# Last pair of heads of a mixed convolution/attention layer: projection units cut in halves earlier and spread over more steps

## What is computed

```
z = u_lat @ w_in                              # B, C, X, G (1024 columns each), Q, K, V, BG
y_a = z[B] * dwconv(z[C] * z[X], w_conv, 1)   # short convolution over tokens
y_a = y_a * silu(z[G])
y_b = neighbourhood_attention(q, k, v, k_ctx, v_ctx, rpb) * silu(z[BG])
y_lat = concatenate([y_a, y_b]) @ w_out
```

## Time and profile before

| | |
|---|---|
| median of 3 runs | 2403.7 us (2403.24 to 2404.94) |
| the profiled execution's own time | 2403.63 us |
| its span in the trace | 2401.8 us |
| PE busy | 2261.0 us, 94% |
| DVE, ACT, POOL busy | 63%, 49%, 22% |
| step 5 of the last pair to the end of its block | 1222 to 1291.5 us |

### The profile page before, as it was taken

One profiled execution on the slowest core, in us unless ns is written; L12 is line 12 of the kernel. 1 busy time (PEld: TensorE's weight loads), 2 busy tenths in 40 slices (PEclk: granted clock), 3 DMA queues, 4 the chain that ended last, 5 costly groups with the idle time before them and its releaser, 6 DMA issues. The chain is left out here.

```text
span 2401.8 us, 33875 instructions
## 1 busy us (share of the span) xinstructions
PE 2261.0 (94%) x12000; PEld 1966.3 (82%) x12000; DVE 1501.9 (63%) x2368; ACT 1188.4 (49%) x1714; POOL 528.3 (22%) x303
## 2 busy tenths in 40 slices
PE   4799999999999999999997999799999999995998
PEld 3688888888888888888885888688998999894887
DVE  5167575774757757576576436557766776667444
ACT  4244434444344443444444334366777678767322
POOL 1333132331322313223230300022212221220300
PEclk8899999999999999999998999899999999997999
DMA  6212211221112211122116555111111111114654
GB/s 247 62 35 68 63 57 33 68 72 59 57 33 73 71 55 57 33 81 63 55 27 226 163 167 175 55 40 53 53 52 54 53 53 58 48 53 140 218 154 144
DMA packets 165352, 199.79 MB, mean 83 GB/s; under 512 B 51064, under 2 KB 125944, under 8 KB 162168
## 3 DMA queue, kind: packets, MB, share of 16 engines
q1 hardware_dynamic: 155304, 174.53, 23.2%
q10 hardware_dynamic: 9792, 23.07, 2.7%
q0 software_dynamic: 144, 0.52, 0.1%
HBM read 166.11 MB, written 31.98 MB: 82 GB/s over the span
## 5 line engine op out<-in xcount | busy, mean ns | idle before, releaser
L950 PE MATMUL ps<-u_hi,w_hi 128*128 128x512 f32 (+1 forms) x1536 | 559.5, 364 | 16.6 <-POOL w_lo L637 16.6
L950 PE MATMUL ps<-u_hi,w_lo 128*128 128x512 f32 (+1 forms) x1536 | 545.2, 355 | 0.0
L950 PE MATMUL ps<-u_lo,w_hi 128*128 128x512 f32 (+1 forms) x1536 | 544.1, 354 | 0.0
L950 PEld LDWEIGHTS ps<-u_hi,w_hi 128*128 128x128 f32 x1536 | 290.6, 189 | 54.1 <-POOL w_lo L637 16.7
L950 PEld LDWEIGHTS ps<-u_hi,w_lo 128*128 128x128 f32 x1536 | 290.3, 189 | 41.9
L950 PEld LDWEIGHTS ps<-u_lo,w_hi 128*128 128x128 f32 x1536 | 291.2, 190 | 37.3
L1525 POOL TENSOR_TENSOR o_w_lo<-o_w_raw,o_w_hi 128x1024 fp32r<-128x1024 f32 x48 | 138.8, 2891 | 669.5 <-ACT o_w_hi L1540 669.5
L1795 PE MATMUL ps<-u_hi,o_w_hi 128*128 128x426 f32 (+2 forms) x640 | 238.0, 372 | 13.9 <-POOL o_w_lo L1525 9.3
L742 ACT ACTIVATE probs<-probs,neg_max 128x640 f32<-128x640 f32 (+1 forms) x160 | 122.8, 768 | 251.5 <-DVE neg_max L858 250.4
L637 POOL TENSOR_TENSOR w_lo<-w_stage,w_hi 128x1024 fp32r<-128x1024 f32 x64 | 153.4, 2397 | 418.6 <-ACT w_hi L695 418.6
L656 POOL TENSOR_TENSOR bias_tile<-bias_piece,col_mask 128x384 f32<-128x384 f32 x128 | 142.7, 1118 | 440.0 <-DVE neg_max L858 439.9
(11 more groups left out here) (176 smaller groups left out, 4274.6 us busy)
## 6 DMA issues: line engine op xcount, KB each, us to landing
y_tile<-y_scratch SPq DMA_DIRECT2D x72, 512.0 KB, 5.1
w_stage<-in_w_even SPq DMA_DIRECT2D x64, 512.0 KB, 3.7
o_w_raw<-in_w_odd SPq DMA_DIRECT2D x48, 512.0 KB, 3.6
ada_piece<-in_w_ada SPq DMA_DIRECT2D x16, 1024.0 KB, 5.7
wout_raw<-in_w_out SPq DMA_DIRECT2D x16, 1024.0 KB, 10.1
ada_pieces<-in_w_ada SPq DMA_DIRECT2D x4, 2048.0 KB, 18.3
y_scratch<-h_backward SPq DMA_DIRECT2D x16, 512.0 KB, 2.7
h_scratch<-h_tile ACTq DMA_DIRECT2D x18, 256.0 KB, 2.3
```

The lines of the kernel that those rows point to most:

```text
L950: last = nc.tensor.matmul(ps[:, bank(j, g), 0:t - f], w[:, slot, c * P:(c + 1) * P], x[:, c, f:t], start=(c == 0 and n == 0), stop=(c == K ...
```

## The change

For the last pair alone: whole units in steps 0 to 4 instead of 0 to 7, half units (4 of the 8 chunks) in steps 5 to 18 instead of 8 to 15. Step 19 has none. The convolution store moves from step 16 to step 19.

```diff
+LAST_WHOLE = 5
...
-        if s < 8:
+        if s < LAST_WHOLE:
             return [(*ORDER[s], 0, KC)]
-        if s < LAT_STEPS:
-            return [(*ORDER[8 + (s - 8) // 2], s % 2 * (KC // 2), (s % 2 + 1) * (KC // 2))]
+        if s < STEPS - 1:
+            n, part = divmod(s - LAST_WHOLE, 2)
+            return [(*ORDER[LAST_WHOLE + n], part * (KC // 2), (part + 1) * (KC // 2))]
         return []
...
-                    if s == (LAT_STEPS if last else 13):
+                    if s == (STEPS - 1 if last else 13):
                         act.wait_ge(ya_done, i + 1)
                         store_conv(act, i)
```

## The result

| | before | changed |
|---|---|---|
| median | 2403.47 us (2402.37 to 2404.94, 6 runs) | 2412.51 us (2410.36 to 2413.4, 6 runs) |
| the profiled execution's own time | 2403.63 | 2412.11 |
| mean granted clock of PE | 0.977 | 0.974 |

The ratio is 1.0033 with a 95% interval of 1.0023 to 1.0042: the change costs 9.0 us. The forecast was 6.3 us more, 2409.9. The direction and the place were right; the time is 2.6 us above the forecast and 0.7 us above the upper end of the range that the prediction gave.

A forecast was written before the change was run, and what follows sets the result against it. PE, busy for 94% of the span, bounds the kernel; DVE's last output and its store set the block's end. Exposed loads delay the border 6.3 us: 2403.63 + 6.3 = 2409.9 us, range 2406.3 to 2411.8.

The forecast's parts named there:

- main term: Block's border: CG2 done 7.0 us later, the weight loads' transfer exposed, and the block left 6.3 us later.
- 15.45 to 16.8: Block's border: us from CG2's end, when the loads are issued, until all stores have landed.
- The step keeps its 7.66: Step 7: DVE's L841 meets POOL's split of G's weights again, so the step takes 7.66 us, as step 6 did before.
- rival 3: Step 7: POOL's next bias tile runs first after the split, DVE waits 1.1 us more; 2411.0 us, chance 0.10.
- Steps 8, 9 and 10: 3 x 4.58: Steps with halves of CB0 and CB1 take 4.58 us each, 13.74 in all.
- the steps' gain: Last pair: weigh(19) comes at 1284.55 instead of 1286.30, 1.75 us earlier.
- On SP's queue behind them: Block's border: the attention store, issued at about 1287 behind the four loads on SP's queue, waits for them.
- From the same state ... at half its clock: Behind the border: work starts in the same order and state, PE at half clock, so 6.3 us carry to the end.
- Rival 1: Block's border: the store of y does not wait for the loads, the kernel is 1.75 us faster; 2401.9 us, chance 0.07.
- rival 2: Step 7: L841 begins before POOL's split, so the step takes 5.9 us instead of 7.66; 2408.1 us, chance 0.12.
- Rival 4: Last pair: steps come out 1.5 to 3 us shorter in all than forecast; 2407 to 2408.4 us, chance 0.11.
- steps 12, 16 and 17: Last pair's steps without a profile row of their own, taken as 4.1, 3.9 and 4.05 us.

The follow-up runs named there:

- before_late_loads: The kernel before, steps untouched, with SP issuing the four output weight loads only after output(17): 2411.11 us, ratio 1.0027.
- lw7: The changed kernel with whole units in steps 0 to 6, halves in steps 7 to 16, convolution store in step 17: 2404.27 us, ratio 0.9999 to the kernel before.
- split_late: The changed kernel with POOL's split of G's weights behind bias tile 10 instead of 8 in the last pair: 2410.86 us, ratio 1.0028.
- act_store: The changed kernel with the last pair's attention store issued on ACT's queue instead of SP's: 2411.7 us, ratio 1.0035.
- lw7_two_p1late: lw7 with two of four loads behind the next block's first y load, the next four behind y of tiles 2 and 3: 2401.3 us, ratio 0.9989.

## Why the prediction was right, and where it was off

- **The main term held.** CG2 done later, the loads later, their transfer exposed, the block left later. before_late_loads brings 7.4 of the 9.0 us with this alone by the medians, 5.9 of 9.3 by its trace; lw7, whose loads come 52.33 us behind weigh(5) where before it was 51.85, loses nothing. "15.45 to 16.8" for the time to the last landing was 15.83.
- **"The step keeps its 7.66" was mis-sized.** It was 8.27, as rival 3 had said: the bias tile was ready when the split ended and met the two L845. They took 1.73 us instead of the 1.01 that split_late shows without POOL beside them. The Trainium skill, "SBUF — State Buffer", section "SBUF: two separate sides", gives operations of DVE with two SBUF inputs as ones that can be kept waiting by GpSimd; the 1.73 agrees, and this is the case of three in a row that the trace of before did not have. The price was 0.6 to 0.7, not the 1.1 of the rival.
- **"Steps 8, 9 and 10: 3 x 4.58" failed for step 8,** 6.20. I had seen that the smaller filling becomes idle time in step 7, and had costed that idle time at nothing. It was 3.52 us, and the clock fell behind it. Steps 9 and 10 were 4.48 and 4.49.
- These two make the loads 8.8 us late instead of 7.0, and the border 7.86 instead of 6.3. They also ate the steps' gain: 0.08 us instead of 1.75.
- **"On SP's queue behind them" was wrong as a mechanism,** and that its number held is luck. The rows that I took it from, 11.5 us behind four loads against 2.4, tell a full DMA from an idle one as well as a full queue from an empty one. act_store told them apart.
- **"From the same state ... at half its clock" held, but the same course did not follow.** Both begin the block at 0.50. Before, the clock was back at 1.00 by the first output product, at 1298; in the changed kernel it stayed at 0.50 until 1310. That is about 2 us by the first tile, and by the other traces it could have gone either way. Of it and the border's delay some 0.8 us came back, 0.38 of it as before's wait for the third tile's y went away: this is what the prediction had named as a way to be wrong, and it is small.
- **Rival 1** fell with the landing of 10.6 us, **rival 2** with L843's 2.43. **Rival 4** fell: steps 12, 16 and 17, without rows of their own, were 0.1 to 0.2 us shorter than I had them.

As a sum: 6.3 forecast, plus 1.6 at the border from steps 7 and 8, plus 2 from the clock behind it, less 0.8 given back in the second and third tiles, less 0.8 by which this execution was ahead at weigh(5), is 8.3; the span is 8.5 us longer.

What stays open: why before_late_loads has two groups of times; when the clock at the border comes back in time for the first output product, and so what share of the 9.0 us it is (0.7 us in the one pair of traces that can be compared, but no run held the clock); what the convolution store's move from step 16 to step 19 costs (its 0.66 MB at 378 GB/s would be 1.7 us, an estimate from the earlier trace rows, and no run moved it alone); and whether the store lands late for shared bandwidth or because its report waits for earlier writes.

## What to carry to other kernels

Follow a moved piece of work to the transfers that wait for it: here every microsecond by which CG2 came later was one by which 4 MB of loads came later, and the steps' gain could not reach the end past them, as lw7 shows. A stretch that is short of DMA gives back at its next wait what is saved at one, so ask where the moved bytes collide next (3 us in the third tile). Count both traces from a common point ahead of the change: the executions here differ by up to 2.4 us at weigh(5), as much as the gains that are looked for. And idle time that a smaller filling leaves on PE is not free even off the path, if PE needs its full clock right behind it.

## What the runs showed of the hardware that was not expected

- PE's idle of 3.52 us inside the steps was followed by a granted clock of 0.71 and 0.50 for 4 us, and cost 1.6 us, in five executions out of five (2.7 us in one of them); idles of 0.71 and 1.62 us in the same place (split_late) left it at 1.00.
- After the longer idle at the block's border, 3.54 to 14.77 us, the clock was full by the first output product in eight of fourteen traces and half in six, with idles of 6.53 us on both sides; the half clock made the first tile 2.1 to 2.2 us longer in the change and in lw7_two_p1late.
- A small store's landing followed the bytes in flight, not its queue: 2.4 us with the loads nearly done, 5.4 with two loads issued 5.2 us before it, 10.6 with four on its own queue, 10.2 with four on the other. The convolution stores, first on their queue, took 2.7 us with no loads in flight and 7.6 to 10.2 with four.
- A one-input operation of DVE took 0.35 us alone on 128x256 and 0.55 on 128x640, and either took 2.43 to 2.63 us beside POOL's split of 2.35 to 2.40 us, wherever the split was put.
